# Expert positions in couples beside the mixer's steps, in the three heavy tiles of a two-layer GLA, mLSTM, SSD and PEER kernel

## The reference

```
u = ln(x) * (1 + sc1) + sh1
p = u @ w_in                                  # 3136 columns: heads, gates, convolution channels
heads = GLA scan | mLSTM scan | SSD scan      # chunked, forward and backward
x = ln(ALPHA * x + g1 * (rms_norm(heads) * gnorm_w) @ w_out) * ln1_w + ln1_b
u = ln(x) * (1 + sc2) + sh2                   # PEER, the channel mixer
s = (u @ wq) . keys  ->  top 16 of 128, twice, per head; top 16 of the 256 sums -> idx, g
act = gelu(sum_d peer_u[idx, d] * u[d]) * g   # 8 heads x 16 experts = 128 rows a token
x = ln(ALPHA * x + g2 * sum_k act[k] * peer_v[idx[k]]) * ln2_w + ln2_b
```

## Time and profile before

| | us |
|---|---|
| median of 3 runs | 4716.02 (4712.96 to 4717.74) |
| profiled execution, its own time | 4717.43 |
| its span, first to last instruction | 4715.6 |
| busy: PE / DVE / POOL / ACT | 3592.0 / 3127.2 / 2104.0 / 1091.2 |
| DMA | 1607.93 MB, mean 341 GB/s |

### The profile page before, as it was taken

How to read it: one execution, slowest core, us unless ns; L and a number is a source line. 1 busy time by engine, 2 the same in 40 slices (tenths; PEclk the granted TensorE clock), 3 DMA queues, 4 the chain that set the end, 5 groups by cost and what they waited for, 6 DMA issues and landing times.

```text
span 4715.6 us, 39891 instructions
## 1 busy us (share of the span) xinstructions
PE 3592.0 (76%) x11372; PEld 1868.3 (40%) x11372; DVE 3127.2 (66%) x7065; ACT 1091.2 (23%) x2759; POOL 2104.0 (45%) x1816
## 2 busy tenths in 40 slices
PE   8872978766977877976567598866697797797776
PEld 3430466532432432433444247643243242343222
DVE  1236757776686686685768575876668668668555
ACT  1100233311212212212421223531221222222211
POOL 0101655535444344445756555553534344445443
PEclk9886987888999998998779798778899899999999
DMA  8564886778999999999988978675999999999998
GB/s 298 189 237 175 307 317 220 247 283 338 388 400 420 376 407 421 376 409 391 362 339 329 355 284 307 223 279 213 371 370 414 420 364 414 418 368 415 422 421 351
DMA packets 368478, 1607.93 MB, mean 341 GB/s; under 512 B 48417, under 2 KB 89633, under 8 KB 245377
## 3 DMA queue, kind: packets, MB, share of 16 engines
q0 software_dynamic: 241920, 1342.28, 72.5%
q1 hardware_dynamic: 126240, 262.99, 15.1%
q10 hardware_dynamic: 96, 0.10, 0.0%
HBM read 1568.02 MB, written 37.20 MB: 340 GB/s over the span
## 4 chain that ended last, share of the span: by engine, by line
PE 33%; DVE 26%; DMA 25%; issue 7%; SPq 3%; POOL 3%; ACT 2%; DVEq 0%; ACTq 0%; POOLq 0%
DMA big<-in_experts,big 19%; PE bank L2060 14%; DVE big L1453 8%; PE bank L1808 3%; PE bank L2034 3%; PE bank L1803 3%; PE bank L1757 2%; PE bank L2005 2%; POOL big L2180 2%; DMA big<-in_w_in 2%; DVE big L1439 2%; DVE big L1352 1%; DVE big L1354 1%; DVE big L1351 1%; ACT big L1706 1%
## 5 line engine op out<-in xcount | busy, mean ns | idle before, releaser
L2060 PE MATMUL bank<-big 128*128 128x512 f32 x4416 | 2162.4, 639 | 616.7 <-ACT big L1706 578.9
L1453 DVE CUSTOM_DVE_ANT_0 big<-big 128x1024 f32<-128x1024 f32 x1280 | 1550.9, 1232 | 543.3 <-DMA big<-in_experts,big 488.5
L2180 POOL DMA_INDIRECT big<-in_experts,big x880 | 1015.7, 1154 | 1335.4 <-PE bank L2060 1203.3
L2060 PEld LDWEIGHTS bank<-big 128*128 128x128 f32 x4416 | 862.5, 203 | 1850.4 <-issue 1082.6
L2186 POOL DMA_INDIRECT big<-in_peer_v,big x400 | 495.9, 1240 | 437.0 <-PE bank L2060 200.7
L2177 POOL DMA_INDIRECT big<-in_peer_u,big x400 | 464.7, 1162 | 441.3 <-DVE big L1411 190.7
L1706 ACT ACTIVATE big<-big 128x128 f32<-128x128 f32 x1104 | 389.1, 395 | 825.2 <-DVE big L1424 709.1
L1712 ACT ACTIVATE big<-big 128x2 f32<-128x2 f32 x640 | 130.0, 204 | 1412.8 <-DVE big L1453 1396.2
L1808 PE MATMUL bank<-big 128*128 128x256 f32 x960 | 229.1, 401 | 40.0 <-DMA big<-in_w_in 38.8
L1764 PE MATMUL bank<-big 128*128 128x128 f32 x240 | 46.8, 360 | 263.5 <-DVE big L1016 147.1
L1439 DVE SCALAR_TENSOR_TENSOR big<-big 128x1024 f32<-128x1024 f32 x173 | 222.8, 1288 | 10.1 <-DVE big L1439 1.5
(11 more groups left out here) (245 smaller groups left out, 3166.3 us busy)
## 6 DMA issues: line engine op xcount, KB each, us to landing
big<-in_w_ada SPq DMA_DIRECT2D x24, 2048.0 KB
big<-in_w_in SPq DMA_DIRECT2D x48, 1024.0 KB, 8.8
big<-modd SPq DMA_DIRECT2D x34, 512.0 KB, 21.6
big<-in_w_out SPq DMA_DIRECT2D x16, 1024.0 KB, 17.6
big<-in_peer_wq SPq DMA_DIRECT2D x16, 1024.0 KB, 26.9
big<-in_experts,big POOLq DMA_INDIRECT x880, 10.7
y_d<-big SPq DMA_DIRECT2D x20, 512.0 KB, 7.0
big<-y_d SPq DMA_DIRECT2D x20, 512.0 KB, 11.1
```

What stands on the lines that cost most here:

```text
L1453: v_.tensor_tensor_reduce(ring[:, j, 0:D], ring[:, j, 0:D], EU[it % 2], 1.0, 0.0, ALU.mult, ALU.add, DOT[:, n % 16:n % 16 + 1]).then_inc(e ...
L2060: i = mm(ps[4 + h][:, :], DG[:, q % DIAGS * P:(q % DIAGS + 1) * P], ring[:, n % RING, D + 512 * h:D + 512 * h + 512], start=first, stop=last)
L2180: g_.indirect_dma_start(ring[:, n % RING, :], None, io["experts"], offset(N)).then_inc(e_gat[n % RING], 16)
```

## The change

`spread_over` gets an argument `by`. With 2 it takes the events two at a time: both stand behind each other, and the mixer ticks ahead of them are those up to the couple's middle, so that a stretch is twice as long. `order_of_work` passes 2 for the expert tiles 0, 4 and 5. `apart` only moves up in the file. Where the count is odd (tiles 4 and 5: 51 and 53), the last one stands alone. Everything else is as before: what is issued, at which position, on which engine; only `summed_by_vector` reads the new order, and there pair 26 of tile 0 now stands behind a scan tick and pair 44 behind an output tick.

```
-def spread_over(order, first, last, events):
+def spread_over(order, first, last, events, by=1):
     ws = [TICKS[i][1] for i in range(first, last + 1)]
     total, acc, i = sum(ws), 0.0, 0
-    for e, ev in enumerate(events):
-        goal = total * (e + 0.5) / len(events)
+    for e in range(0, len(events), by):
+        goal = total * (e + by / 2) / len(events)
...
-        order.append(ev)
+        order.extend(events[e:e + by])
     order.append(("m", last))
...
-            spread_over(order, first, last, [("e", it, g) for g in range(g0, g1)])
+            spread_over(order, first, last, [("e", it, g) for g in range(g0, g1)], 2 if apart(it) else 1)
```

More of the change, by code:

```diff
@@ L125, in spread_over, with apart @@
             order.append(("m", t))
-        order.append(ev)
+        order.extend(events[e:e + by])
     order.append(("m", last))
+def apart(it):
+    return it in (0, 4, 5)
 def order_of_work():
@@ L160 @@
 ORDER = order_of_work()
-def apart(it):
-    return it in (0, 4, 5)
 def stands_at(near, far, end):
```

## The result

The changed kernel takes 4774.9 us (median of 4 runs, 4748.6 to 4793.3) against 4714.8 us for the kernel before on the same chip; the ratio is 1.0123, 95% interval 1.0068 to 1.0177, +58 us. The forecast was 4727, the range ended at 4760: the sign was right and the size was not. The profiled execution took 4793.3 us, the upper end of the four runs; its 76 us over the profile of before are more than the median shows, so I use its rows for where time went and the ratios for how much.

What follows compares the result with a forecast made beforehand. No single bound; beside the mixer, the mixer sets the time, its waits split between TensorE, VectorE and DMA. Scans +16, joints 0, projection 0, sums -2.5, tables -3 give +10.5 on 4717.43: 4728, median 4727 us; range 4692 to 4760.

Steps and rivals of the forecast that it cites:

- The scans: Between scan ticks of tiles 0, 4 and 5, 20 VectorE covers are lost: +16 us, between 0 and 42.
- one in two as useful: In the scans, half the 20 lost covers matter at 2.1 us a hop: 21 us, less 5 for longer couples.
- the lower end of 0: In the scans, no net cover: tile 0 has two positions more than tile 5, its scan 12.5 us longer.
- The joints: Where stages meet in tiles 0, 4 and 5, gains and losses sum to +0.2, put at 0, from -14 to +14.
- The couple behind the barrier of tile 0: Between the scan's barrier and first sums, it lies in front of the starting state's landing from memory: -5 us.
- the output product: Output stage: tile 0's couple moves ahead of the transposes, covering only 2.9 us, +4.7; tile 5 -1.
- the loads: Output stage's loads: tile 0 has a couple in front in place of one, -3.8 us; tile 5 none, +3.8.
- the query product: Output stage: the couple covers more of VectorE's wait, -2 us in tile 5, -1.5 in tile 4, 0 in tile 0.
- The projection: Input projection: positions ahead of each convolution and eviction change by at most one, cost 0 us.
- lumps on VectorE: Rival: couples of 10.2 us delay SyncE's weight blocks for TensorE in the projections; slower, 4752 us, chance 0.16.
- Tables: ACT's gelu in three tiles: a couple's second gelu finds its table loaded, loads from 78 to about 45, -3 us.
- Sums: Vector sums of pairs 26 and 44: two sums of 1.29 us leave VectorE, -2.5 us.

Runs made afterwards that it cites:

- its own experiment: Couples only beside the output stages, single positions elsewhere, against the kernel before: ratio 1.0010 (0.9996 to 1.0023), +5 us.
- the bad couples: Kernel before with couples beside the scans directly ahead of k5 and k13, where VectorE hardly waited: ratio 1.0159 (1.0137 to 1.0180), +75 us.
- the bad singles: Kernel before with single positions beside the scans directly ahead of k5, k7, k9 and k13: ratio 1.0054 (1.0035 to 1.0073), +25 us.

## Why the prediction was wrong, by its own steps

**The scans, the term that failed: +16 predicted, +41 measured.** The mechanism was right: covers lost on VectorE. What failed is the size, at the step "one in two as useful" at 2.1 us each. The prediction's own upper end, 20 x 2.1 = 42 us, is near the value by luck: the count is too high, since the places at the four long steps fell by 12 and not by 20, and the price per hop is too low. The waits at the four lines grew by 28.8 us in the profile of the couples beside the scans, which took 27.2 us longer than that of before; the median is +41. Three readings made the forecast small. First, 2.1 us was the mean of five waits, several of them remainders behind a position that covered part; the longest with nothing under them are 3.9 and 5.4 us (after, L1168 and L1251). Second, "one in two useful" took the usefulness as a constant; it is a matter of the step, and the coupled list has 8 of 21 places at the four long steps where the list before had 20 of 42. Counting that needed only the list and the waits by line. Third, the lower end of 0 came from comparing tiles 0 and 5, which differ in their joints too.

**The joints, 0 predicted.** The couple behind the barrier of tile 0 was to be worth -5, lying in front of the same landing. VectorE's timeline there (start, duration, idle before in brackets):

```profile
681.80 0.16 DVE L1424 TENSOR_TENSOR big<-big 128x2 f32<-128x2 f32 x1 [18.14 <-SPq L404]
...
691.83 0.31 DVE L1156 COPY big<-bank 128x153 f32<-128x153 f32 x1
...
705.27 0.47 DVE L1173 TENSOR_TENSOR_SCAN big<-big 4x128 f32<-4x128 f32 x1 [8.98 <-DMA big<-in_state]
```

The couple is 10.0 us, with two sums at each position and not one, and TensorE's sums for L1156 were ready at 685.6: it held the first step up by 6.2 us. The starting state was not the same landing either. SyncE's issue of it, before and after:

```profile
691.03 0.43 SPq L839 DMA_DIRECT2D big<-in_state  x1
```
```profile
693.10 0.43 SPq L839 DMA_DIRECT2D big<-in_state  x1
```

VectorE had it 5.2 us after the issue before (696.26) and 12.2 after it here. In the 12.8 us from just ahead of that issue the gathers moved 800 packets where they had moved 570. Two other traces bear on it. With couples in VectorE's queue alone the gathers moved 574 packets in such a window and the state was there 5.6 us after its issue (699.60 to 705.18 us); with couples beside the scans in all queues it was 785 packets and 9.8 us (688.52 to 698.27). So it is not VectorE's couple that delays the landing but what the other queues do with theirs, and the couple's gathers, which share the DMA with this load, are the likely cause. The barrier itself was 1.1 us later, so a gain of 5 was a loss of about 8.

In the output stages of tile 0 both rows moved as foretold in sign, the output product more weakly and the loads more strongly, and the query product the other way:

```profile
DVE big L1320 <- PE bank L2005: 15.6, 1, 15.6
DVE big L1369 <- PE bank L2034: 11.4, 1, 11.4
...
DVE big L1289 <- DMA big<-in_gnorm_w: 2.6, 1, 2.6
```

The output product's 13.0 is 15.6 (20 foretold), the loads' 13.4 is 2.6 (10 foretold), since VectorE came to it at 948.0 us and not at 927.1. The query product took 8.9 before and takes 11.4: the couple's value products stand in TensorE's queue between the query's own (7.0 us of L2060 between two groups of L2034, from 1011.0 us on), where I had the couple as VectorE's cover only (0 to -2 in each tile). From L1366 to L1369 the three tiles took 9.6, 13.2 and 10.6 us before, 10.6, 14.7 and 10.8 with couples in VectorE's queue alone, and 17.3, 17.8 and 18.2 with couples in all. That stage is the +5 of its own experiment, with 0 inside the interval.

**The projection, 0 predicted, +11.** The counts of positions ahead of each tick were right: they change by at most one. The failed step is that this one was priced at nothing. It is 5.0 us of VectorE ahead of a piece for which ACT and then TensorE wait, and the piece came 4.0 us later in tile 0. How much of the +11 this is, no run separates. The rival "lumps on VectorE" had the wrong partner (a weight block), and the lump of 10 us that it feared lay there before as well; its 4752 is nearer than my forecast for another reason than the one it gave.

**Tables, -3 predicted.** 78 loads in the three tiles became 21 + 15 + 22 = 58, not 45, and with fewer of them ACT's queue in couples was 14 us slower: no saving is shown. In the rows a load costs its 1.28 us and nothing beside it: in the change's profile one begins at 555.10 us, 0.02 after the activation ahead of it ended, and the gelu behind it starts at 556.39, so that the 100 us for 78 loads are the measure here and not 207. **Sums**: two fewer, as foretold (x173 to x171). **Light tiles** unchanged, as foretold (the last one 319.3 and 319.6 us). **The time of the three tiles** rose above 1833 us, so the forecast's own test of its sign held; its test on the projections (8 us) failed: tile 0's went from 251.8 to 261.1 us, 6.2 of the 9.3 being the couple at the barrier, and tile 5's, counted from the tile's start, from 298.0 to 309.6.

## What to carry to other kernels

In this kernel a filler (work that can stand anywhere, here a position) beside a chain of hops between engines was worth mainly the wait that lay under it: list the waits of the waiting engine by line, count how many fillers stand directly ahead of the long ones, and only then price a change of spacing. Take the price from the longest bare waits of a line and not from the mean, which holds remainders. When fillers are joined, follow the joined piece through all queues: its products stand in TensorE's, and its gathers share the DMA with the loads of the next stage. And a count that changes by one is not nothing: one more filler ahead of a piece that two engines wait for makes the piece late by its length.

## What the runs showed of the hardware

The granted clock fell where TensorE's waits grew. In the window above TensorE had stood 11.3 us, its granted clock was 0.50 there, the lower of the two levels, and 1.00 before and behind it; in the window of the same times before it was 1.00. The four transposes behind the wait took 1.12 us where they had taken 0.66. In the scan of tile 5 the same number of products was busy for 187.2 us at 0.80, 204.3 at 0.74 and, with the bad couples, 219.8 at 0.70. Busy time times clock is nearly the same in all three (150, 151 and 154 us), so the clock accounts for the longer matmuls, which I had not priced. It does not follow VectorE's waits alone: with the bad singles these grew too (43.4 us at the four lines in that scan, 21.4 before), and the clock stayed at 0.80 (193.0 us busy).

The same kernel scattered by 45 us (changed, 4 runs) and by 28 (before, in its largest set of 25 runs), more than a single profile can be trusted for: the profile of the kernel with couples beside the projection was taken in its fastest run, 4712 us, and does not show its +11.
